# Head norms of two outputs computed with DVE's statistics instructions, one instruction per head, in place of wide passes

## What is computed

```python
def group_norm_heads(z, eps):
    mu = jnp.mean(z, axis=-1, keepdims=True)
    var = jnp.mean(jnp.square(z - mu), axis=-1, keepdims=True)
    return (z - mu) * lax.rsqrt(var + eps)
...
y = group_norm_heads(y, RW_GN_EPS) * lnx_w.reshape(H, N) + lnx_b.reshape(H, N)   # 8 heads of 64
...
o = group_norm_heads(o, RET_GN_EPS).reshape(B, T, RET_V_WIDTH)                   # 8 heads of 128
return jax.nn.silu(g) * o
```

## Time and profile before

| | us |
|---|---|
| median of 3 runs | 1051.25 |
| lowest and highest run | 1050.33, 1058.77 |
| profiled execution | 1057.03 |
| its span in the trace | 1055.2 |
| PE busy | 963.6 |
| DVE busy | 692.3 |
| ACT busy | 528.3 |

### The profile page before, as it was taken

The page is one execution under the profiler, slowest core; times in us unless marked ns, Lnnn a source line. Parts: engine busy times, 40 slices in busy tenths (PEclk is TensorE's granted clock), DMA queues, the critical chain, the costliest instruction groups (busy, mean ns, idle before and its releaser), DMA issues.

```text
span 1055.2 us, 14425 instructions
## 1 busy us (share of the span) xinstructions
PE 963.6 (91%) x5761; PEld 838.2 (79%) x5761; DVE 692.3 (66%) x945; ACT 528.3 (50%) x785; POOL 62.3 (6%) x65
## 2 busy tenths in 40 slices
PE   4989999999989979999997998898897988789898
PEld 4887897888868769999886998777776867667676
DVE  4579636863887678888636867755554767765555
ACT  4654322232543456655435557647653565543453
POOL 6002312310000000000000000000000000000000
PEclk9899999999999989999998999999998999889899
DMA  9442222122544546555554454422223444420042
GB/s 297 125 143 93 81 76 85 41 81 82 168 149 160 164 138 198 187 175 197 191 173 157 122 163 153 144 103 80 81 89 120 149 141 165 155 79 1 1 160 80
DMA packets 80531, 135.78 MB, mean 129 GB/s; under 512 B 3893, under 2 KB 46225, under 8 KB 80336
## 3 DMA queue, kind: packets, MB, share of 16 engines
q1 hardware_dynamic: 78640, 131.37, 38.0%
q0 software_dynamic: 1824, 3.48, 1.1%
HBM read 133.79 MB, written 1.05 MB: 128 GB/s over the span
## 4 chain that ended last, share of the span: by engine, by line
PE 56%; ACT 9%; DVE 8%; issue 5%; DMA 1%; DVEq 0%; ACTq 0%
PE bank L421 15%; PE bank L423 15%; PE bank L422 15%; ACT upper L1142 3%; PE bank L409 3%; DVE lower L1603 2%; PE bank L1002 1%; PE bank L1017 1%; PE bank L994 1%; ACT arena L1204 1%; PE bank L835 1%; ACT arena L1446 1%; ACT L1446 1%; DVE arena L2077 1%; DMA loaded<-in_ffn_w_up 1%
## 5 line engine op out<-in xcount | busy, mean ns | idle before, releaser
L1603 DVE TENSOR_TENSOR lower<-loaded,upper 128x2048 fp32r<-128x2048 f32 (+1 forms) x123 | 279.1, 2276 | 161.9 <-ACT upper L1142 159.9
L1142 ACT ACTIVATE upper<-loaded 128x2048 fp32r<-128x2048 f32 (+1 forms) x123 | 233.0, 1899 | 144.8 <-PE bank L423 123.6
L421 PE MATMUL bank<-xT_upper,upper 128*128 128x256 f32 x656 | 188.8, 288 | 9.7 <-DVE xT_lower L1644 9.7
L422 PE MATMUL bank<-xT_lower,upper 128*128 128x256 f32 x656 | 187.0, 285 | 0.0
L423 PE MATMUL bank<-xT_upper,lower 128*128 128x256 f32 x656 | 186.8, 285 | 0.0
L421 PE MATMUL bank<-upper,xT_upper 128*128 128x512 f32 (+1 forms) x368 | 151.0, 410 | 9.2 <-DVE lower L1603 6.7
L423 PE MATMUL bank<-upper,xT_lower 128*128 128x512 f32 (+1 forms) x368 | 145.2, 395 | 0.0
L422 PE MATMUL bank<-lower,xT_upper 128*128 128x512 f32 (+1 forms) x368 | 144.2, 392 | 0.0
L421 PEld LDWEIGHTS bank<-xT_upper,upper 128*128 128x128 f32 x656 | 127.6, 195 | 11.5 <-issue 11.5
L1204 ACT ACTIVATE arena<-bank 128x512 f32<-128x512 f32 (+1 forms) x95 | 54.0, 587 | 160.4 <-PE bank L634 62.7
L421 PE MATMUL bank<-upper,split_arena 128*128 128x512 f32 x296 | 122.8, 415 | 11.0 <-DVE split_arena L1644 4.5
(11 more groups left out here) (306 smaller groups left out, 1258.8 us busy)
## 6 DMA issues: line engine op xcount, KB each, us to landing
loaded<-in_w_in SPq DMA_DIRECT2D x27, 1024.0 KB, 5.2
loaded<-in_ffn_w_up SPq DMA_DIRECT2D x22, 1024.0 KB, 5.2
loaded<-in_ssm_in_w SPq DMA_DIRECT2D x20, 1024.0 KB, 5.3
loaded<-in_ffn_w_down SPq DMA_DIRECT2D x11, 1024.0 KB, 5.0
loaded<-in_ssm_out_w SPq DMA_DIRECT2D x8, 1024.0 KB, 5.0
loaded<-in_ple_gate_w SPq DMA_DIRECT2D x8, 1024.0 KB, 5.1
loaded<-in_attn_in_w SPq DMA_DIRECT2D x8, 1024.0 KB, 5.2
loaded<-in_w_branch_ret SPq DMA_DIRECT2D x4, 1024.0 KB, 5.0
```

The lines of the kernel that those rows point to most:

```text
L421: mm(out, a[0], b[0], start=start, stop=False)
L422: mm(out, a[0], b[1], start=False, stop=False)
L1142: A(part(upper, PARTS, n), part(loaded, LOADS, n), ACT.Copy).then_inc(uppers, 1)
L1603: TT(part(lower, LOADS, n), part(loaded, LOADS, n), part(upper, PARTS, n).bitcast(F32), sub) \
```

## The change

`centre` is written anew and loses the operand for squares and the number of heads. For each head of each tile one `bn_stats` on the head's 64 or 128 elements writes six numbers, and one `bn_aggr` makes a mean and a variance of them. One `tensor_scalar` then adds epsilon to all variances. After the root and the reciprocal, one `tensor_scalar` for each head subtracts the mean and multiplies by the reciprocal root in the same instruction, both as operands of one number per partition. The separate products L1944 and L1951 are gone. `y_rows` is now raised by 2 from the last of the 16 head instructions.

```diff
+        parts6, moments = sm(200, 2, 48), sm(296, 2, 16)
...
-            def centre(x, sq, tiles, n, w, eps, count):
+            def centre(x, tiles, w, eps, count):
...
-                for i in tiles:
-                    ins = ve.tensor_reduce(mean[:, i, 0:n], x[:, i, :, :], AX.X, add)
-                link(ins)
-                both_ = slice(tiles[0], tiles[-1] + 1)
-                link(TS(mean[:, both_, 0:n], mean[:, both_, 0:n], 1.0 / w, None, mul))
-                for i in tiles:
-                    ins = TT(x[:, i, :, :], x[:, i, :, :], bc(mean[:, i, 0:n].unsqueeze(2), P, n, w), sub)
+                both_ = slice(tiles[0], tiles[-1] + 1)
+                for i in tiles:
+                    for hd in range(8):
+                        ins = ve.bn_stats(parts6[:, i, 6 * hd:6 * hd + 6], x[:, i, hd, :])
                 link(ins)
                 for i in tiles:
-                    ins = TT(sq[:, i, :, :], x[:, i, :, :], x[:, i, :, :], mul)
+                    for hd in range(8):
+                        ins = ve.bn_aggr(moments[:, i, 2 * hd:2 * hd + 2], parts6[:, i, 6 * hd:6 * hd + 6])
                 link(ins)
-                for i in tiles:
-                    ins = ve.tensor_reduce(var[:, i, 0:n], sq[:, i, :, :], AX.X, add)
-                link(ins)
-                TS(var[:, both_, 0:n], var[:, both_, 0:n], 1.0 / w, eps, mul, add).then_inc(sem("gn_var"), 1)
+                mv = moments.rearrange("p i (h two) -> p i h two", two=2)
+                TS(var[:, both_, 0:8], mv[:, both_, :, 1], eps, None, add).then_inc(sem("gn_var"), 1)
                 ve.wait_ge(sem("gn_root"), count)
-                link(ve.reciprocal(rs8[:, both_, 0:n], rs8[:, both_, 0:n]))
+                link(ve.reciprocal(rs8[:, both_, 0:8], rs8[:, both_, 0:8]))
+                for i in tiles:
+                    for hd in range(8):
+                        ins = TS(x[:, i, hd, :], x[:, i, hd, :], moments[:, i, 2 * hd:2 * hd + 1], rs8[:, i, hd:hd + 1], sub, mul)
+                return ins
...
-            centre(x, by_head(ar(19472, 2, 512), 64), (0, 1), 8, 64, 64e-5, 1)
-            for i in range(2):
-                TT(x[:, i, :, :], x[:, i, :, :], bc(rs8[:, i, 0:8].unsqueeze(2), P, 8, 64), mul).then_inc(sem("y_rows"), 1)
+            centre(x, (0, 1), 64, 64e-5, 1).then_inc(sem("y_rows"), 2)
...
-                centre(x, by_head(ar(19472, 2, D), P), (i,), 8, P, 1e-5, 2 + i)
-                link(TT(x[:, i, :, :], x[:, i, :, :], bc(rs8[:, i, 0:8].unsqueeze(2), P, 8, P), mul))
+                link(centre(x, (i,), P, 1e-5, 2 + i))
```

More of the change, by code:

```diff
@@ L1882, in _ @@
                 dense(("y", n))
-            def centre(x, sq, tiles, n, w, eps, count):
+            def centre(x, tiles, w, eps, count):
+                both_ = slice(tiles[0], tiles[-1] + 1)
                 for i in tiles:
-                    ins = ve.tensor_reduce(mean[:, i, 0:n], x[:, i, :, :], AX.X, add)
-                link(ins)
-                both_ = slice(tiles[0], tiles[-1] + 1)
-                link(TS(mean[:, both_, 0:n], mean[:, both_, 0:n], 1.0 / w, None, mul))
-                for i in tiles:
-                    ins = TT(x[:, i, :, :], x[:, i, :, :], bc(mean[:, i, 0:n].unsqueeze(2), P, n, w), sub)
+                    for hd in range(8):
+                        ins = ve.bn_stats(parts6[:, i, 6 * hd:6 * hd + 6], x[:, i, hd, :])
                 link(ins)
                 for i in tiles:
-                    ins = TT(sq[:, i, :, :], x[:, i, :, :], x[:, i, :, :], mul)
+                    for hd in range(8):
+                        ins = ve.bn_aggr(moments[:, i, 2 * hd:2 * hd + 2], parts6[:, i, 6 * hd:6 * hd + 6])
                 link(ins)
+                mv = moments.rearrange("p i (h two) -> p i h two", two=2)
+                TS(var[:, both_, 0:8], mv[:, both_, :, 1], eps, None, add).then_inc(sem("gn_var"), 1)
+                ve.wait_ge(sem("gn_root"), count)
+                link(ve.reciprocal(rs8[:, both_, 0:8], rs8[:, both_, 0:8]))
                 for i in tiles:
-                    ins = ve.tensor_reduce(var[:, i, 0:n], sq[:, i, :, :], AX.X, add)
-                link(ins)
-                TS(var[:, both_, 0:n], var[:, both_, 0:n], 1.0 / w, eps, mul, add).then_inc(sem("gn_var"), 1)
-                ve.wait_ge(sem("gn_root"), count)
-                link(ve.reciprocal(rs8[:, both_, 0:n], rs8[:, both_, 0:n]))
+                    for hd in range(8):
+                        ins = TS(x[:, i, hd, :], x[:, i, hd, :], moments[:, i, 2 * hd:2 * hd + 1], rs8[:, i, hd:hd + 1], sub, mul)
+                return ins
             def by_head(a, w):
```

## The result

| | before | changed |
|---|---|---|
| median of 10 runs, us | 1054.03 | 1061.20 |
| lowest and highest, us | 1050.33, 1060.20 | 1060.32, 1065.67 |
| profiled execution, its span, us | 1057.03, 1055.2 | 1060.32, 1058.5 |
| ratio, 95% interval | | 1.0086, 1.0061 to 1.0111 |

A forecast was written before the change was run, and what follows sets the result against it. TensorE was taken as the bound, so only DVE work behind the roots counts: 1.9 (y) + 0.85 (tile 0) = +2.8 us on the median 1051.25, giving 1054.0 us; 8-in-10 range 1050.5 to 1059.0.

The forecast's parts named there:

- (a): Narrow head instructions on DVE: 0.206 us start to start at 64 columns, 0.249 at 128; 53 ns per operand.
- cheap operands: Rival: a head instruction's two scalars cost nothing beside its columns; +0.2 us, 1051.5 us; chance 0.18.
- dear narrow instructions: Rival: head instructions at L1959's pace, statistics at the scan's; +6.4 us, 1057.7, or +4.7 without overlap; chance 0.15.
- (b): y ahead of the root: statistics and aggregations take 4.2 us, variance at 275.3; gain nothing, 1.4 us more idle DVE.
- (e): Tile 0 ahead of the root: the passes saved turn into a longer wait for ACT; gain nothing.
- (c): y behind the root: sixteen head instructions (3.38 us) replace two products (1.29 us); TensorE waits +1.9 us at the transposes.
- (d): Whether y's shift carries: ACT's copy and root move with TensorE; the 3.47 us wait does not swallow the 1.9 us.
- (f): Tile 0 behind the root: head instructions (2.08 us) replace one product (1.23 us), ahead of TensorE's split; +0.85 us.
- (g): Tile 1: about 1.5 us shorter (2.3 less ahead of the root, 0.85 more behind); TensorE gains nothing.
- (h): TensorE's clock: nothing lost behind the new wait, the old wait's loss unchanged; bounds -1.7 and +2 us.
- The faster rival: Shorter statistics reach TensorE if ACT takes tile 0's root before its copy; -3.2 us, 1048.0; chance 0.03.

The follow-up runs named there:

- e5_changed_again: The changed kernel run again without alteration for a second trace, against the kernel before: median 1061.43 us, ratio 1.0031 (0.9999 to 1.0063).
- e1_y_only: Only the y norm is new, the retention output keeps the old wide passes; against the kernel before: median 1060.31 us, ratio 1.0037 (1.0004 to 1.0071).
- e9_changed_root_early: The changed kernel with ACT's root of tile 0 moved ahead of yT's last gate copy; against the kernel before: median 1054.59 us, ratio 0.9965.
- e12_changed_third: The changed kernel run a third time without alteration, against the kernel before: median 1059.55 us, ratio 1.0072 (1.0037 to 1.0107).

## Why the prediction was right in kind and wrong in size

- (a) Price of a head instruction: forecast 0.206 and 0.249 us from start to start, measured 0.223 and 0.257. Right to 8%. The rivals "cheap operands" and "dear narrow instructions" are both out. By the sentence that the prediction cites from the Trainium skill, VectorE: DVE Perf Modes, section "The DRAIN you can't avoid", y's 16 instructions would have taken 16 x 0.308 = 4.9 us, an estimate; they took 3.66, so this trace disagrees with that sentence again. The section goes on that an instruction which is not held starts earlier; the prediction left that out, and the overlaps here, 0.308 - 0.223 = 0.085 and 0.340 - 0.257 = 0.083 us, are such an earlier start.
- (b), (e) Ahead of the roots: forecast nothing, and nothing it was. The statistics cost 0.127 us at 64 columns and 0.195 at 128, the aggregation 0.068; statistics and aggregation together are at most 0.26 us, near the 0.24 taken. DVE's wait for the roots grew to 10.9 us, not 8: 9.3 in e5_changed_again, where the clock did not drop at y, and 1.6 more here, because the drop delayed ACT's second root.
- (c) y behind the root: forecast +1.9 us, measured a wait of 2.06.
- (d) The shift carries through to the second wait: right, shown by e1_y_only, with the wait for the split at 3.48 us as before and the stretch 2.27 us longer.
- (f) Tile 0 behind the root: forecast +0.85 us, measured 4.39 - 3.47 = +0.92.
- (g) Tile 1 costs TensorE nothing: right, no wait of TensorE above 0.25 us between 306.86 and 356.21. Its size was put wrongly, without effect: 2.3 us is what the new passes ahead of the root were taken to cost, not what they save. From its first pass to the end of the head instructions tile 1 took 5.2 us on DVE, where it took 7.1, so 2.0 less and not 1.5.
- (h) The clock is the step that failed: "I take nothing for it" behind the new wait, and "its loss as it is" behind the longer one. It was sized from one wait of 2.3 us with a full clock behind it. The same trace has a wait nearer in length to the 1.9 us forecast, of 1.95 us ending at 782.77, and the 6 us behind it have a mean granted clock of 0.72:

```profile
782.77:788.77 6.00, 5.79 (x18) 3.98 (x19) 3.70 (x8) 2.90 (x10) 0.00 (x0) 0.72 0.00 0
```

  Three traces of the changed kernel lost 2.9, 0.2 and 2.9 us to the clock. The upper bound of 2 us, for one more drop, was too low as well: in the two that lost 2.9, 1.7 are the drop at y and 1.2 a longer one behind the split. What makes the clock drop in one execution and not in the next stays open.
- The base. The forecast stood on the median of three executions, 1051.25. Ten of them have a median of 1054.03, and 119 average 1056.1. Of the 7.2 us by which 1061.2 exceeds the forecast of 1054.0, 2.8 are the base of this comparison, about 2.2 what the stretch lost beyond the forecast (5.0 - 2.8; 2.0 of it is the clock, 0.2 the waits), and the last 2.2 what this comparison, at +7.2 us in its medians, shows beyond the 5.0.
- The spans of the first two traces, 1055.2 and 1058.5, differ by 3.3 us and seem to confirm the forecast. They do so by chance, as the next section but one shows.
- The faster rival named the right lever: the root's place on ACT. It did not decide, as ACT's list was unchanged; with the root moved, e9_changed_root_early is 0.35% faster than before, and its stretch 2.5 us shorter, where the rival had 3.2.

## What to carry to other kernels

Before trading wide passes for narrow ones, ask on which side of the last wait each stands: here 32 cheap instructions ahead of a root that ACT had not yet taken gained nothing, and 16 dearer ones behind it cost TensorE 2 us. Price an instruction with two operands per partition about 0.12 us above one with constants, and look for work that can fill a wait before making the work ahead of that wait shorter. A wait on TensorE costs its length and, in some executions, a clock drop beside it, here 1.7 us as a rule and up to 3 us; a range for one has to hold both, and the base has to come from more than three executions.

## What was not expected of the hardware

**The length of a wait does not tell whether the clock drops.** The mean granted clock in the 6 us behind some of TensorE's waits, in all of the 14 traces that have the wait:

| wait, us | place | traces with the clock at 0.78 or less |
|---|---|---|
| 1.85 | about 721 us | 11 of 14, all 0.72 |
| 1.95 | about 783 us | 14 of 14, all 0.72 |
| 2.06 | the transposes of y | 3 of 6, at 0.72; the others 1.00 |
| 2.32 | about 669 us | 2 of 14 |
| 2.60 | about 805 us | 1 of 14, at 0.50 |
| 3.4 | about 649 us | 7 of 12 |
| 3.5 | the split, before | 3 of 3, at 0.72 |
| 4.39 | the split, changed | 4 of 4, from 0.52 to 0.75 |
| 4.6 | about 378 and 575 us | 28 of 28, at 0.50 |

A mean of 0.72 is 0.28 x 6 = 1.7 us of a full clock lost, one of 0.50 is 3 us. Why 1.95 us always and 2.32 hardly ever is not settled; what TensorE did ahead of the wait differs at the two places, and no run here varied it. The drop at y came in 2 of the 3 traces of the changed kernel itself, so it is not the kernel alone that decides.

**The clock also drops without a wait.** In each of the 14 traces it falls between 600 and 635 us, while TensorE is busy for all of the 35 us. Its mean over them is 0.95 in eight traces, 0.90 in four and 0.85 in two, that is 1.7, 3.5 and 5.2 us of full clock. Of the first trace of the changed kernel, and then of before:

```profile
620.00:630.00 10.00, 10.00 (x48) 10.00 (x49) 3.38 (x8) 0.00 (x0) 0.00 (x0) 0.50 0.42 135
```

```profile
620.00:630.00 10.00, 10.00 (x75) 10.00 (x76) 5.07 (x10) 5.10 (x6) 0.00 (x0) 0.83 0.46 135
```

What sets the length of this drop was not tested.

**A second pace at full clock.** The feed-forward's products, between the waits of 4.6 us near 378 and 575 us, take 192.4 to 193.8 us in nine traces and 197.3 to 197.9 in five, whatever the kernel. The granted clock from 410 to 560 us is 1.00 in all 14. The rows of the same 20 us count 172 products at the slow pace (before, e12_changed_third) and 179 at the fast one (the first trace of the changed kernel). Of before:

```profile
420.00:440.00 20.00, 20.00 (x172) 20.00 (x171) 17.68 (x28) 11.46 (x17) 0.00 (x0) 1.00 0.56 181
```

and of the changed kernel:

```profile
420.00:440.00 20.00, 20.00 (x179) 20.00 (x179) 17.98 (x29) 12.90 (x19) 0.00 (x0) 1.00 0.55 176
```

That is 4 to 5 us in an execution, and what sets it stays open.

**Why the first two spans agreed with the forecast.** The trace of before had the slow pace (197.43 us) and that of the changed kernel the fast one (193.31), which gave back 4.1 of the 5.9 us. But what follows, up to the wait near 650 us, took 4.1 us more in the changed kernel (78.10 against 74.04), mainly by the longer drop near 620 us; from there to the wait near 670 us it lost 1.4 more, and behind 918 us it gained 3.0 back, with smaller differences elsewhere. That all of them sum to 3.3 us is chance. In the third trace of the changed kernel what lies outside the stretch nearly cancels, and the spans differ by 1061.1 - 1055.2 = 5.9 us, as much as its stretch.

**The clock and the spread.** Over 109 executions of the kernel before, a mean granted clock lower by 0.01 goes with a time longer by 6.4 us (a straight line through their times and clocks); it leaves 2.3 us of scatter out of 4.2. So most of the spread from execution to execution goes with how much of the time the clock was low. That the clock is its cause is argued from this line and not shown by a run that changed it.
